# Another order for the paired products of a feed-forward layer, and the linear attention's scores in two groups of two heads

## What is computed

```python
def gla_chunked(q, k, v, log_a):        # 4 heads, DK = 64, DV = 128, chunks of 64 tokens
    b = jnp.cumsum(log_a, axis=-2)
    q_i = q * jnp.exp(b)
    k_i = k * jnp.exp(-b)
    scores = jnp.einsum('nbhck,nbhsk->nbhcs', q_i, k_i)
    scores = jnp.where(causal, scores, 0.0)
    o_intra = jnp.einsum('nbhcs,nbhsv->nbhcv', scores, v)
    ...                                 # o_inter = q_i times the states before each chunk
# first_block
    o = rmsnorm(gla_chunked(q, k, v, log_a), gla_norm_g[l]) * jax.nn.silu(p_g)
    o_conv = c_b * causal_depthwise_conv(c_c * c_h, conv_w[l])
    x = x + jnp.concatenate([o_gla, o_conv], axis=-1) @ w_out[l]
    h2 = rmsnorm(x, norm2_g[l])
    ffn = (jax.nn.silu(h2 @ w_ffn_gate[l]) * (h2 @ w_ffn_up[l])) @ w_ffn_down[l]    # D_FF = 2816
    x = x + ffn
```

## Time and profile before

| | us |
|---|---|
| median of 3 runs | 2495.06 |
| lowest and highest | 2494.91, 2496.38 |
| the profiled execution, whole | 2494.21 |
| its span, first to last instruction | 2492.5 |
| mean granted clock of PE | 0.987 of full |

### The profile page before, as it was taken

One profiled execution on the slowest core, in us unless ns is written; L12 is line 12 of the kernel. 1 busy time (PEld: TensorE's weight loads), 2 busy tenths in 40 slices (PEclk: granted clock), 3 DMA queues, 4 the chain that ended last, 5 costly groups with the idle time before them and its releaser, 6 DMA issues.

```text
span 2492.5 us, 29802 instructions
## 1 busy us (share of the span) xinstructions
PE 2416.4 (97%) x11248; PEld 1987.4 (80%) x11248; DVE 1239.6 (50%) x1655; ACT 804.3 (32%) x1173; POOL 644.1 (26%) x332
## 2 busy tenths in 40 slices
PE   8999999899999989999999999999999999999997
PEld 6888788678888878888888888877877877878886
DVE  4444673844444443344321102477777787753534
ACT  4422132333233321134211101255555555541221
POOL 2221122345555522222221122111121121122221
PEclk9999899999999999999999999999999999999998
DMA  3111222132222242212222224332322323344223
GB/s 129 43 43 34 85 79 90 66 138 85 92 78 76 77 152 102 85 60 85 101 93 76 78 99 140 100 98 94 118 91 86 110 84 100 110 152 143 92 95 109
DMA packets 66148, 234.63 MB, mean 94 GB/s; under 512 B 7936, under 2 KB 8080, under 8 KB 66064
## 3 DMA queue, kind: packets, MB, share of 16 engines
q1 hardware_dynamic: 51376, 179.98, 22.1%
q10 hardware_dynamic: 14688, 53.48, 5.3%
HBM read 175.76 MB, written 57.67 MB: 94 GB/s over the span
## 4 chain that ended last, share of the span: by engine, by line
PE 93%; DVE 4%; issue 1%; DMA 1%; ACT 1%; DVEq 0%; SPq 0%; POOL 0%; ACTq 0%
PE dense L683 22%; PE dense L685 22%; PE dense L684 22%; PE dense L831 5%; PE dense L833 5%; PE dense L832 5%; PE aux L956 2%; PE aux L940 2%; PE aux L941 1%; PE aux L969 1%; PE aux L968 1%; PE aux L903 1%; DVE residual L1733 1%; DVE att_p_lo L1924 1%; PE aux L713 0%
## 5 line engine op out<-in xcount | busy, mean ns | idle before, releaser
L683 PE MATMUL dense<-x_hi,w_hi 128*128 128x512 f32 x2000 | 809.4, 405 | 14.2 <-DVE x_lo L1487 13.0
L685 PE MATMUL dense<-x_hi,w_lo 128*128 128x512 f32 x2000 | 783.5, 392 | 0.0
L684 PE MATMUL dense<-x_lo,w_hi 128*128 128x512 f32 x2000 | 782.4, 391 | 0.0
L584 POOL TENSOR_TENSOR w_lo<-w_raw,w_hi 128x1024 fp32r<-128x1024 f32 x157 | 382.5, 2436 | 1414.0 <-ACT w_hi L1028 1405.9
L1028 ACT CAST w_hi<-w_raw 128x1024 fp32r<-128x1024 f32 x156 | 163.9, 1051 | 886.2 <-PE dense L685 863.2
L683 PEld LDWEIGHTS dense<-x_hi,w_hi 128*128 128x128 f32 x2000 | 378.1, 189 | 84.9 <-issue 15.3
L685 PEld LDWEIGHTS dense<-x_hi,w_lo 128*128 128x128 f32 x2000 | 377.0, 188 | 81.5
L684 PEld LDWEIGHTS dense<-x_lo,w_hi 128*128 128x128 f32 x2000 | 378.5, 189 | 67.6 <-issue 1.2
L1528 DVE TENSOR_TENSOR work<-dense,rstd 128x1024 f32<-128x1024 f32 x95 | 116.0, 1221 | 401.1 <-PE dense L685 395.2
L619 POOL TENSOR_TENSOR w_lo<-w_sums,w_hi 128x512 fp32r<-128x512 f32 x80 | 122.2, 1539 | 142.8 <-ACT w_hi L1180 142.8
L683 PE MATMUL dense<-work_split,w_hi 128*128 128x512 f32 x352 | 138.0, 392 | 1.1 <-DVE work L1785 1.1
(11 more groups left out here) (236 smaller groups left out, 3318.1 us busy)
## 6 DMA issues: line engine op xcount, KB each, us to landing
w_raw<-weights SPq DMA_DIRECT2D x177, 512.0 KB, 3.8
kept_qkv<-work ACTq DMA_DIRECT2D x24, 512.0 KB, 2.6
kept_m<-work ACTq DMA_DIRECT2D x22, 512.0 KB, 2.6
work<-kept_m SPq DMA_DIRECT2D x22, 512.0 KB, 3.5
w_raw_b<-weights SPq DMA_DIRECT2D x20, 512.0 KB, 4.3
residual<-xT SPq DMA_DIRECT2D x16, 512.0 KB, 6.6
kept_x<-residual ACTq DMA_DIRECT2D x16, 512.0 KB, 2.7
att_q<-kept_qkv SPq DMA_DIRECT2D x32, 256.0 KB, 4.0
```

Of the source, the lines that this page charges most:

```text
L584: pool.tensor_tensor(WL[:, u.slot], WR[:, u.slot], WH[:, u.slot].bitcast(f32), ALU.subtract).then_inc(w_lo, 1)
L683: pe.matmul(dst, WH[:, u.slot, k], hi, start=(k == 0), stop=False)
L684: pe.matmul(dst, WH[:, u.slot, k], lo, start=False, stop=False)
L685: last = pe.matmul(dst, WL[:, u.slot, k], hi, start=False, stop=(k == nk - 1))
```

## The change

Four things are done together.

1. `DIRECT` becomes 6 and `DUOS` 19: three tiles are made by ordinary units, 19 by pairs. `U_DOWN` stays 77.
2. The hand-over from the units to the pairs is ordered anew. The weight sums of pair 0 move behind the fifth unit's scaling, the splits of the input sums all go to VectorE (one was POOL's), the fourth `lo_again` moves behind three joins of pair 0, the banks change (B7, B5 in slot 1, B1, B6 in slot 0), `half` shifts by one at pairs 4, 8 and 12, even pairs use `WR` and odd ones `WRB`. At the end four tiles are asked for before the next weights instead of two, and `m_lo` is spread between the joins.
3. `work` and `residual` are placed ahead of the weight buffers in SBUF.
4. The GLA scores are made in two groups, heads 0 and 1 after unit 12, heads 2 and 3 after unit 17, the matmuls alternating between the two halves of the partitions (and two pairs of banks of `aux`). Outputs and norm sums of the later heads move by one unit.

```diff
-U_GU, TILES, DIRECT, DUOS = 33, 22, 4, 20
+U_GU, TILES, DIRECT, DUOS = 33, 22, 6, 19
+T_DUO = DIRECT // 2
...
-AT_SCORES = (12, 14, 16, 18)
-AT_O = (13, 15, 17, 19)
-AT_NORM = (14, 16, 18, 20)
+AT_SCORES = (12, 17)
+AT_O = (13, 15, 18, 20)
+AT_NORM = (14, 16, 19, 21)
...
-        B7, B5, B1, B6 = 0, 1, 2, 3
+        B7, B5, B1, B6 = 2, 3, 0, 1
...
         def half(p, i):
-            return (7 * p + i + 2) % 4
+            return (7 * p + i + 2 + min(p // 4, 3)) % 4
...
         def w_pair(p):
-            return WR if p % 2 else WRB
+            return WRB if p % 2 else WR
...
# SyncE
-            load_m(0)
-            load_m(1)
+            for t in range(4):
+                load_m(t)
             sp.wait_ge(w_sum, 4 * DUOS)
             sp.wait_ge(d_lo, 6 * DUOS)
...
-            for t in range(2, 8):
+            for t in range(4, 8):
                 load_m(t)
...
# POOL
-                    if p == 0 and i == 1:
-                        pool.wait_ge(t_hi, 3)
-                        pool.tensor_tensor(TX[:, 2, 1], XSUM[:], TX[:, 2, 0].bitcast(f32), ALU.subtract
-                                           ).then_inc(t_lo_pool, 1)
...
# PE
-            def scores(h):
-
-                rows = slice(h % 2 * DK, (h % 2 + 1) * DK)
-                if h == 0:
+            def scores(j):
+
+                if j == 0:
                     pe.wait_ge(st_c, 4 * (NCH - 1))
                     pe.wait_ge(gd, GD_ALL)
                 else:
-                    pe.wait_ge(sc_cp, h)
+                    pe.wait_ge(sc_cp, 2)
+                    pe.wait_ge(o_rd, 2)
                 for b in range(NBLK):
                     tok = slice(b * P, (b + 1) * P)
-                    last = pe.matmul(PA[:, b // 4, b % 4 * P:(b % 4 + 1) * P], WK[rows, U_K + h // 2, tok],
-                                     WK[rows, U_Q + h // 2, tok], start=True, stop=True)
+                    for p in range(2):
+                        rows = slice(p * DK, (p + 1) * DK)
+                        last = pe.matmul(PA[:, 2 * p + b // 4, b % 4 * P:(b % 4 + 1) * P], WK[rows, U_K + j, tok],
+                                         WK[rows, U_Q + j, tok], start=True, stop=True)
                 last.then_inc(sc_mm, 1)
...
-                                g15=[lambda: spread(2, WK[:, TMP + 3])]))
+                                g12=[lambda: spread(2, WK[:, TMP + 3])]))
...
                 if p:
                     pe.wait_ge(joined, 4 * p)
                 else:
+                    pe.wait_ge(evac, U_DUO - 1)
                     pe.wait_ge(t_lo, 1)
                 times(p, 0, TX[:, 0, 0], TX[:, 0, 1], B7, True)
...
# ScalarE, from the input sums to the last half of pair 0
+            split(Unit(U_GU + 4))
+            silu_gate(1)
+            hi_sum(2, XSUM[:])
+            split(Unit(U_GU + 5))
+            store_m(1)
             hi_half(0, 0)
             hi_half(0, 1)
-            silu_gate(1)
-            hi_sum(2, XSUM[:])
+            silu_gate(2)
             hi_half(0, 2)
...
# VectorE, the last pair
                 if p == DUOS - 1:
-                    for t in range(4):
-                        m_lo(t)
+                    m_lo(0)
+                    m_lo(1)
                 dve.wait_ge(prod, 6 * p + 4)
                 dve.wait_ge(p1_kept, p + 1)
                 dve.tensor_tensor(UB[:], UB[:], bank(B6), ALU.add).then_inc(joined, 1)
...
+                if p == 0:
+                    lo_again(3, 1, 1)
                 if p < DUOS - 1:
                     weight_sums(p + 1)
                 else:
-                    m_lo(4)
+                    m_lo(2)
+                    m_lo(3)
...
```

More of the change, by code:

```diff
@@ L206, in two_blocks @@
         XL = place("x_lo", [KT, S], f32r)
+        WK = place("work", [20, S])
+        XR = place("residual", [KT, S])
+        wk, xr = at["work"], at["residual"]
         WR = place("w_raw", [2, KT, P])
@@ L348, in half, with held @@
         def half(p, i):
-            return (7 * p + i + 2) % 4
+            return (7 * p + i + 2 + min(p // 4, 3)) % 4
+        def held(p, i):
+            same = [r for r in range(7 * p + i) if half(r // 7, r % 7) == half(p, i)]
+            return (same[-1] // 7, same[-1] % 7) if same else None
         def w_pair(p):
-            return WR if p % 2 else WRB
+            return WRB if p % 2 else WR
         def quarter(p, i):
@@ L607, in _ @@
                 if u - 2 in AT_SCORES:
[L608 to L612, removed]
+                    for h in (2 * AT_SCORES.index(u - 2), 2 * AT_SCORES.index(u - 2) + 1):
+                        pool.wait_ge(sc_cp, h + 1)
+                        pool.affine_select(out=SC[:, h % 2], in_=SC[:, h % 2], compare_op=ALU.is_ge, fill=0.0,
+                                           base=0, pattern=[[0, NBLK], [1, P]], channel_multiplier=-1
+                                           ).then_inc(sc_sel, 1)
             splits(U_OUT + 2, U_DUO - U_OUT - 2)
@@ L850, in _ @@
                 else:
+                    pe.wait_ge(evac, U_DUO)
                     pe.wait_ge(b_lo, 1)
@@ L1106, in _ @@
                 if u in AT_SCORES:
-                    h = AT_SCORES.index(u)
-                    act.wait_ge(sc_sel, h + 1)
-                    act.wait_ge(gd, GD_ALL)
-                    q = WK[CHUNK * (h % 2):CHUNK * (h % 2 + 1), U_Q + h // 2].rearrange("p (b e t) -> p e b t", e=2, t=CHUNK)
-                    for e in range(2):
-                        last = act.copy(SC[rows_s(e), h % 2, :, rows_v(e)], q[:, e])
-                    last.then_inc(q_put, 1)
+                    for h in (2 * AT_SCORES.index(u), 2 * AT_SCORES.index(u) + 1):
+                        act.wait_ge(sc_sel, h + 1)
+                        act.wait_ge(gd, GD_ALL)
+                        q = WK[CHUNK * (h % 2):CHUNK * (h % 2 + 1), U_Q + h // 2].rearrange(
+                            "p (b e t) -> p e b t", e=2, t=CHUNK)
+                        for e in range(2):
+                            last = act.copy(SC[rows_s(e), h % 2, :, rows_v(e)], q[:, e])
+                        last.then_inc(q_put, 1)
                 if u - 1 in AT_NORM:
@@ L1169, in hi_half @@
             def hi_half(p, i):
-                q = 7 * p + i
-                if q < 4:
-                    act.wait_ge(mm_done, U_DUO - 1 + q // 2)
+                if held(p, i) is None:
+                    act.wait_ge(mm_done, U_DUO - 1 + i // 2)
                 else:
-                    act.wait_ge(*product((q - 4) // 7, (q - 4) % 7, prod, mm_done))
+                    act.wait_ge(*product(*held(p, i), prod, mm_done))
                 if i in (0, 1, 3, 6):
@@ L1666, in _ @@
                 if u in AT_SCORES:
-                    gla_scores(AT_SCORES.index(u))
+                    for p in range(2):
+                        gla_scores(2 * AT_SCORES.index(u) + p)
                 if u in AT_NORM:
@@ L1782, in _ @@
                 if p == DUOS - 1:
-                    m_lo(5)
+                    m_lo(4)
                 dve.wait_ge(mm_done, U_DUO + 2 * p + 2)
```

64 lines of the change are left out of this document (34 added, 30 removed).

## The result

| | before | changed |
|---|---|---|
| median of the runs, us | 2494.98 (2487.03 to 2496.38) | 2456.18 (2455.22 to 2458.66) |
| span of the profiled execution, us | 2492.5 | 2455.4 |
| granted clock, mean | 0.987 | 0.994 |

The ratio is 0.9852 (95% interval 0.983 to 0.9875): 38.8 us faster by the medians, 37.1 us by the two profiled spans. The sign was forecast; the time lies 11.7 us under the forecast and 5 us under the range's low end.

The account below looks back on a forecast made before the run. PE was taken as the bound, gaining only from less PE work or closed waits. FFN -29.0 + 2.5 (two units for a pair) + 3.2 + 1.8 = -21.5, GLA -5.7: -27.2 us, forecast 2467.9 us, range 2461 to 2476.

Parts of the forecast that it names:

- What bounds the kernel, and which holes go: FFN: PE is busy 97% of the span; its waits (20.4 us) and low clock behind them (8.6 us) go, 29.0 us.
- The score groups: GLA scores: four groups taking 9.65 us become two alternating groups taking 3.96 us, a gain of 5.7 us.
- The choice of 62 ns: GLA scores: cost per alternating instruction, half of today's 124 ns, taking the two array halves to work side by side.
- the one alternating row: L759, the only group alternating partition halves: 57 ns per instruction, but loading only 64 columns of weights.
- rival 1: GLA scores: halves do not overlap, 110 to 124 ns per instruction, gain 2.6 to 1.7 us, 2471 to 2472; chance 0.24.
- The hand-over: Direct units to pairs: the 9.7 us wait goes; VectorE running late inside pair 0 costs 3.2 us instead.
- The end: End of the pairs: the 6.3 us wait goes; PE waits 1.8 us for the last add, now behind m_lo(4).
- The GLA wait: GLA norm sums: PE's 3.3 us wait stays, moved to unit 21, because the same VectorE collision recurs at unit 20.
- The moved addresses and the swap of the raw buffers: SBUF placement and raw weight buffers: nothing that a row prices, so no term in the sum.
- rival 4: Dense matmuls: the weight buffers' new place slows each; at 3.7 ns more the time is 2501 us; chance 0.02.

Follow-up runs that it names:

- the pairs' part alone: The kernel before with 19 pairs, 6 direct units, new order, banks and halves, but old placement and old scores: 2470.03 us, ratio 0.9918.
- in blocks: The changed kernel with each score group's matmuls run all in one half of the partitions, then the other, instead of alternating: 2460.55 us, ratio 0.9877.
- the experiment with the small tensors first: The changed kernel with its small tensors placed between x and all the rest, ahead of work, residual and the weight buffers: 2496.07 us, ratio 1.0019.
- the second comparison: The changed kernel run again unchanged, beside the kernel before, on another chip than the first four experiments: 2458.6 us, ratio 0.9868.
- The kernel with the old placement: The changed kernel with work and residual put back at their old place behind the weight buffers, all else kept: 2465.25 us, ratio 0.9898.

## Why the prediction was right in sign and 11.7 us too slow

- **What bounds the kernel, and which holes go.** Right. The 9.7, 3.4 and 6.3 us waits and the three low stretches of the earlier trace rows are gone: 29.0 us, and the pairs' part alone gave -21.0 where its terms were -21.5.
- **The score groups.** Right: 1.99 us for a group, forecast 1.98. The choice of 62 ns from the one alternating row held only because the loops alternate; in blocks rival 1 would have come true at 3.43 us, close to its 3.5.
- **The hand-over.** Right in kind, a little large: 1.9 us instead of 3.2. The joins were ready at 505.3 + 0.7, 13.9 us after the end of the sixth unit (492.1) and not 15.8, since the three splits behind POOL took 8.88 us together, 2.96 each, and not 3.5. So the sixth and seventh products hardly waited, and the next pair's wait was 1.2.
- **The end.** 1.6 us against 1.8, by the mechanism that was named: the add stood behind the fifth `m_lo`.
- **The GLA wait** stayed at 3.3 us, at unit 21, as argued. What stood behind it was mis-sized. I took the dense work's low clock as unchanged, from one stretch of 12.6 us. With the old order there, that stretch had a score group of 3.8 us in two experiments and of 2.05 to 2.2 in four. The earlier trace rows showed one throw of a quantity that varies; it is worth about 4 us (1.7 on the score group, 2.1 on the norm sums and the dense work) and belongs in the range, not in the sum.
- **The step that failed** is "The moved addresses and the swap of the raw buffers: nothing that a row prices". The placement is worth 7.5 us alone (0.9954 to 0.9978), and 8.2 us by the pace in the two traces. It is most of the 9.9 us by which the two spans missed the sum of -27.2. A row did hint at it: rival 4 quotes 229 ns in the pairs against 227 in the units, for the same instruction with nothing to wait for. I used that only as a reason against the change, at a chance of 0.02, and did not ask what the excess was or whether it might go. Rival 4's mechanism was the right one, with the other sign; the experiment with the small tensors first shows that its slower side is real too (2496 us, 40 us lost).
- **The starting point** was one execution on the high side. The forecast counts down from its 2494.2 us; the later medians of the same kernel are 2490.3 to 2491.0. Its long GLA stretch and its low stretch near 60 us make 3.6 us of the table above, which would explain the distance; that they are missing in the later executions is not shown. Against the second comparison's -32.2 us the forecast of -27.2 is 5 us short, which is less than the placement's 7.5.
- **The range** was 2461 to 2476. The kernel with the old placement, 2465.3 us, lies in it, 2.6 us under the forecast.

What stays open: how the cost follows from the distance. Counted from the weights up to the streamed operand, the distance is 320 bytes past a multiple of 512 in the kernel before (`work_split` 2.2 ns slower), 384 with the 64 bytes of padding (6.3 ns), and 192 with the small tensors first, where x lies below the weights (6.6 ns); three points make no rule. The experiments move whole buffers, so they show which distance matters and not what in the memory collides. The table of terms above leaves 1.4 us without a row.

## What to carry to other kernels

When the same instruction, with nothing to wait for, shows two paces in two stages, that difference is a term of the sum, and a change of the memory layout can take it away or spread it. Keep the operand that TensorE streams and its weight buffers at distances that are multiples of 1024 bytes (of those, 7168 and multiples of 4096 were run), put odd-sized small tensors behind the large ones, and look at start-to-start times after every edit of a layout. When two half-height groups of matmuls are independent, alternate them one by one. Before a forecast counts down from one profiled execution, compare several: what the clock does in one of them may not be there in the next.

## What the hardware showed that I had not expected

- **Pace and addresses.** A 128x512 matmul starts every 226.7 to 233.4 ns, by the distance of its two operands in SBUF: 7168 bytes and multiples of 4096 fast, 6976 and 7040 slow, up to 42 us of pace excess in one execution. Behind an operand that is off, even one that is not starts slowly: ten matmuls of 231 ns in the kernel before.
- **A low clock without a wait.** Behind the 32 one-column instructions of L707, 3.6 to 4.9 us in which PE counts as busy, the changed kernel's execution ran at 0.51 for 5.6 us. Nine of the fourteen profiled executions here have that stretch at that place, five have none, and among the five are the kernel before and the changed kernel's second execution. It costs 1.6 to 3.3 us, the one-column instructions' own longer time included. A stretch near 60 us, behind 8 matmuls that use 16 of the 128 partitions (L733), comes and goes in the same way.
- **A low clock of varying length.** Behind the same wait of 3.3 us the granted clock stayed low for some 3 to 12.6 us; behind the pairs' waits of 1.2 and 1.6 us it did not fall (the changed kernel's windows at 512.81 and 857.48 show 1.00). In the attention of the second block PE waits seven times for 1.8 to 1.9 us, and the clock fell behind one or two of the seven in eleven of the fourteen executions and behind none in three. Such a stretch cost 1.7 us (window 1664.90, behind this wait):

```profile
1664.89 0.44 PE L947 MATMUL aux<-att_k_hi,att_q_split 128*128 128x384 f32 x1 [1.92 <-DVE softmax_stats L1926]
```
